# A two-block transformer kernel: modulation chunks of the convolution stage summed on VectorE, and one decay product for each forget head instead of two

## What is computed

```
m = split(silu(c) @ w_mod[1] + b_mod[1], 6)
u = h * (1 + m[1]) + m[0]
b_gate, c_gate, x_in = split(u @ w_in, 3)            # 1024 x 3072
y = (b_gate * conv3(c_gate * x_in)) @ w_out          # 1024 x 1024
h = layer_norm(ALPHA * h + m[2] * y)
f = experts(h * (1 + m[4]) + m[3]);  h = layer_norm(ALPHA * h + m[5] * f)
```

```
cum = cumsum(log_sigmoid(ff + b_f))                  # per head, over tokens
s[t, s'] = q[t].k[s'] / 8 + cum[t] - cum[s']         # then causal softmax, @ v
```

## Time and profile before

| | |
|---|---|
| median of 3 runs | 2254.5 us (2253.36 to 2256.22) |
| profiled execution | 2256.84 us, of which the span of instructions is 2255.0 us |
| mean granted TensorE clock | 0.900 of full |
| TensorE busy | 1791.9 us (79%) |
| VectorE busy | 530.0 us (24%) |
| ScalarE busy | 362.1 us (16%) |
| DMA, mean over the span | 260 GB/s, at most 429 in a slice |

### The profile page before, as it was taken

How to read it: one execution, slowest core, us unless ns; L and a number is a source line. 1 busy time by engine, 2 the same in 40 slices (tenths; PEclk the granted TensorE clock), 3 DMA queues, 4 the chain that set the end, 5 groups by cost and what they waited for, 6 DMA issues and landing times. The chain is left out here.

```text
span 2255.0 us, 27622 instructions
## 1 busy us (share of the span) xinstructions
PE 1791.9 (79%) x11960; PEld 1058.7 (47%) x11960; DVE 530.0 (24%) x1051; ACT 362.1 (16%) x729; POOL 57.5 (3%) x69
## 2 busy tenths in 40 slices
PE   6897666656558977656565569999999999999999
PEld 4454111112017743201111147887588678785785
DVE  0435000001012240100000044242343243413432
ACT  1131000000001010000000012223431022324310
POOL 0000000000000000000000001020000001100000
PEclk8997887878779988878778779999999999999999
DMA  9882999999998567999999943211422232112221
GB/s 405 355 365 84 402 428 428 428 428 428 428 429 372 200 247 313 428 428 428 428 428 422 428 170 141 83 47 65 182 76 87 109 150 76 70 62 112 112 87 45
DMA packets 43503, 586.54 MB, mean 260 GB/s; under 512 B 4913, under 2 KB 5041, under 8 KB 8081
## 3 DMA queue, kind: packets, MB, share of 16 engines
q1 hardware_dynamic: 40464, 574.11, 61.7%
q0 software_dynamic: 2224, 8.31, 0.9%
q10 hardware_dynamic: 720, 2.74, 0.3%
HBM read 584.09 MB, written 1.05 MB: 259 GB/s over the span
## 5 line engine op out<-in xcount | busy, mean ns | idle before, releaser
L1321 PE MATMUL ps<-ring,arena 128*32 128x512 f32 x1536 | 244.6, 769 | 170.2 <-DMA ring<-in_experts 157.4
L1321 PE MATMUL ps<-arena 128*32 128x512 f32 x1536 | 254.8, 801 | 156.5 <-DMA arena<-in_experts 156.5
L1087 PE MATMUL ps<-arena,ring 128*128 128x256 f32 (+3 forms) x1184 | 234.7, 359 | 8.0 <-issue 3.2
L1087 PEld LDWEIGHTS ps<-arena,ring 128*128 128x128 f32 (+2 forms) x1184 | 202.3, 189 | 38.3 <-issue 5.1
L1321 PEld LDWEIGHTS ps<-arena 128*32 128x32 f32 x1536 | 50.3, 130 | 355.9 <-DMA arena<-in_experts 259.0
L1321 PEld LDWEIGHTS ps<-ring,arena 128*32 128x32 f32 x1536 | 48.8, 126 | 351.1 <-DMA ring<-in_experts 220.6
L1417 PE MATMUL ps<-arena,ring 128*128 128x256 f32 x768 | 183.6, 388 | 0.0
L1417 PEld LDWEIGHTS ps<-arena,ring 128*128 128x128 f32 x768 | 142.8, 191 | 29.2 <-issue 9.7
L1440 PE MATMUL ps<-arena,ring 128*128 128x256 f32 x640 | 149.2, 383 | 0.0
L1440 PEld LDWEIGHTS ps<-arena,ring 128*128 128x128 f32 x640 | 121.9, 192 | 26.3 <-issue 10.1
L2064 DVE TENSOR_TENSOR arena<-ps,arena 128x512 f32<-128x512 f32 x16 | 10.3, 686 | 496.6 <-PE ps L1321 496.6
(11 more groups left out here) (331 smaller groups left out, 1898.8 us busy)
## 6 DMA issues: line engine op xcount, KB each, us to landing
ring<-in_experts SPq DMA_DIRECT2D x96, 2048.0 KB, 35.8
arena<-in_experts SPq DMA_DIRECT2D x96, 2048.0 KB, 35.7
ring<-in_stream SPq DMA_DIRECT2D x61, 2048.0 KB, 8.5
arena<-in_stream SPq DMA_DIRECT2D x15, 2048.0 KB, 19.2
ring<-in_stream SPq DMA_DIRECT2D x2, 1696.0 KB, 7.0
gate<-in_b_mod POOLq DMA_DIRECT2D x4, 512.0 KB, 10.8
ring<-in_stream SPq DMA_DIRECT2D x4, 512.0 KB, 4.3
tab<-in_tables_first SPq DMA_DIRECT2D x1, 1729.0 KB, 42.5
```

Source lines behind the costliest of these rows:

```text
L1087: mm = M(dst, lhs(k), rhs(k), start=k == 0, stop=k == n - 1)
L1321: mm = M(bank(b + half)[32 * e:32 * e + 32], x[:, k, 32 * e:32 * e + 32], wk[:, e, half * HALF:(half + 1) * HALF], start=k == 0, stop=k == ...
```

## The change

Two edits that don't touch each other.

**Edit 1, modulation chunks of layer 1's groups `early` and `late`.** `mod_chunk` on TensorE and `mod_part` on ScalarE are gone for these eight chunks. In their place `mod_sum` on VectorE makes `part` = sum over the eight row pieces of piece times condition, in eight instructions of 128x512, each waiting for the one before. `mod_fold` stays, with a matrix of ones. It now marks the tile as consumed. The chunks are put between the projections, in the stream, on TensorE and on VectorE.

**Edit 2, forget heads.** The eight gate rows are doubled (rows 96 to 111). `right` holds -8 cum in the second eight rows and 1 in the first. `left`, in two buffers, has for head u only the rows u and 8+u filled: 8 cum and 1. One matmul `left` x `right` gives 8 (cum[t] - cum[s']). VectorE writes `left` anew for each head, in one instruction on 16 partitions.

```diff
+MOD_BEHIND = (("early", 0, 1), ("early", 1, 2), ("late", 0, 2), ("late", 2, 4), ("late", 4, 6), ("late", 6, 6))
@@ weight_stream
-            modulation("early", 0, 1)
-            for j in (2, 4, 3, 5, 0, 1):
+            for n, j in enumerate((2, 4, 3, 5, 0, 1)):
                 add(("conv_in", j), rows(w["w_conv_in"][0, :, j * HALF:(j + 1) * HALF]))
-                if j == 2:
-                    modulation("early", 1)
-            modulation("late")
+                modulation(*MOD_BEHIND[n])
@@ TensorE, mod_fold
+                summed = g in ("early", "late")
+                pe.wait_ge(*(S("mod_dve").at("sum", l, j, KD - 1) if summed else S("mod_act").at("part", l, j)))
...
+                if summed:
+                    mm.then_inc(used, 1)
@@ TensorE, mixer1
                 turn("mix1", h, 0, ready)
-                mod_chunk(*early[0], fold=False)
                 turned("mix1", 0)
...
                 by_halves(0, slot(first), ut, 1).then_inc(used, 1)
-                mod_chunk(*early[1], fold=False)
-                for c in early:
-                    mod_fold(*c)
+                mod_fold(*early[0])
...
                     mm.then_inc(used, 1)
-                pe.wait_ge(*S("mod_dve").at("gate", *early[-1]))
-                modulation("late")
+                    if n == 2:
+                        pe.wait_ge(*S("mod_dve").at("gate", *early[-1]))
+                    group, first, end = MOD_BEHIND[n]
+                    for c in MOD_GROUPS[group][first:end]:
+                        mod_fold(*c)
@@ VectorE, new
+            def mod_sum(l, j):
+                key = ("mod", l, j)
+                part = parts[mod_half((l, j))]
+                ve.wait_ge(*has_landed(key))
+                before = mod_before((l, j), 2)
+                ve.wait_ge(*(consumed(("mod",) + before) if mod_place(before)[0] in ("early", "late") else S("mod_pe").at("fold", *before)))
+                for k in range(KD):
+                    scale = md["condT"][:, k, 0:1]
+                    if k:
+                        ve.wait_ge(*S("mod_dve").at("sum", l, j, k - 1))
+                        V.scalar_tensor_tensor(out=part, in0=slot(key)[:, k], scalar=scale, in1=part, op0=ALU.mult, op1=ALU.add
+                                               ).then_inc(*S("mod_dve").up("sum", l, j, k))
+                    else:
+                        V.tensor_scalar(part, slot(key)[:, k], scale, None, ALU.mult).then_inc(*S("mod_dve").up("sum", l, j, k))
@@ VectorE, conv1
                 for j in range(8):
+                    if j == 4:
+                        for c in late[1:4]:
+                            mod_sum(*c)
                     ve.wait_ge(*consumed(("conv_in", 4 + j // 4)))
...
+                for c in late[4:]:
+                    mod_sum(*c)
                 ve.wait_ge(*Sv.at("z", 7))
@@ TensorE, attention2, forget heads
-                                sel = T1("ident")[:, FF + u - 8:FF + u - 7]
-                                M(dst, at2["cum"][:, a * P:(a + 1) * P], sel.to_broadcast([P, n]), start=False, stop=False)
-                                mm = M(dst, sel.to_broadcast([P, P]), at2["ncum"][:, 0:n], start=False, stop=True)
+                                if a == 0:
+                                    pe.wait_ge(*Sv.at("left", 1, l, u))
+                                mm = M(dst, at2["left"][:, u % 2, a * P:(a + 1) * P], at2["right"][:, 0:n], start=False, stop=True)
@@ VectorE, forget_gate
-                    V.memset(at2["cum"], 0.0).then_inc(*Sv.up("zero", l, 0))
-                    V.memset(at2["ncum"], 0.0).then_inc(*Sv.up("zero", l, 1))
+                    V.memset(at2["right"], 0.0).then_inc(*Sv.up("zero", l))
...
-                    V.tensor_scalar(at2["cum"][rows], f[:, 3], 8.0, None, ALU.mult).then_inc(*Sv.up("cum", l))
-                    V.tensor_scalar(at2["ncum"][rows], f[:, 3], -8.0, None, ALU.mult).then_inc(*Sv.up("ncum", l))
+                    V.tensor_scalar(at2["right"][rows], f[:, 3], right[:, 0:1], right[:, 1:2], ALU.mult, ALU.add).then_inc(*Sv.up("right", l))
@@ VectorE, attention2
+                def left(u):
+                    ve.wait_ge(*Sv.at("left_zero", l, u % 2))
+                    V.tensor_scalar(at2["left"][rows, u % 2], at2["ff"][rows, 3], T2("with_cum", second_at)[rows, u - 8:u - 7],
+                                    T2("with_one", second_at)[rows, u - 8:u - 7], ALU.mult, ALU.add).then_inc(*Sv.up("left", *K, u))
+                for i in range(2):
+                    V.memset(at2["left"][:, i], 0.0).then_inc(*Sv.up("left_zero", l, i))
+                for u in (8, 9):
+                    left(u)
...
                         V.tensor_scalar(st[:, c:c + 2], st[:, 16:18], -1.0, None, ALU.mult).then_inc(*Sv.up("max", *K, u))
+                        if 8 <= u < 14:
+                            left(u + 2)
```

More of the change, by code:

```diff
@@ L139, in second_tables @@
         _put(parts, at, f"level{n}", (i // (2 * b) == t // (2 * b)) & (i // b + 1 == t // b))
+    row = np.arange(P)[:, None]
+    _put(parts, at, "with_cum", 8.0 * (row == FF + np.arange(H2)[None]))
+    _put(parts, at, "with_one", 1.0 * (row == FF + H2 + np.arange(H2)[None]))
+    _put(parts, at, "right", np.concatenate([-8.0 * (row >= FF + H2), 1.0 * (row // H2 == FF // H2)], 1))
     _put(parts, at, "carry", np.repeat((np.arange(2 * T)[None] % CH != 0), P, 0))
@@ L174, in param_columns @@
         fb = g("fox_b_f")
[L175 removed]
+        col(f"fb{layer}", None if fb is None else np.concatenate([np.zeros(FF, np.float32), fb, fb]), 1, FF + 2 * H2)
         col(f"fq_g{layer}", two(g("fox_q_g")), 1)
@@ L512, in two_block_program @@
         at2.update(xn=sc.take(512), t1=sc.take(512), t2=sc.take(512), score=sc.take(768, 2), prob=sc.take(768, 2),
-                   prob_t=sc.take(768, 2), stat=sc.take(64), cum=sc.take(256), ncum=sc.take(256))
+                   prob_t=sc.take(768, 2), stat=sc.take(64), right=sc.take(256))
+        at2["left"] = at2["sq"][:, :, 0:T]
         at2["ff"] = Scratch(ff_at).take(1024, 4)
@@ L990, in _ @@
             ffn(0)
-            def conv_opening(a):
-                if a:
-                    mod_part(*MOD_GROUPS["early"][0])
-                modulated("mix1", m1["ut"], 1, 0)(a)
-            post_norm(0, 1, conv_opening)
-            mod_part(*MOD_GROUPS["early"][1])
+            post_norm(0, 1, modulated("mix1", m1["ut"], 1, 0))
             for j in range(8):
@@ L1002, in _ @@
                   ).then_inc(*S("conv_act").up("c", j))
-            for c in MOD_GROUPS["late"]:
-                mod_part(*c)
             post_norm(1, 0, modulated("ffn1", ff["ut"], 1, 2))
@@ L1031, in mod_fold @@
                         pe.wait_ge(*S("mod_dve").at("gate", *MOD_GATES[i - 1]))
-                    mm = M(bank(mod_row((l, j))), T1("sum_row0"), part, start=True, stop=True)
+                    mm = M(bank(mod_row((l, j))), T1("ones" if summed else "sum_row0"), part, start=True, stop=True)
                 else:
@@ L1036, in mod_fold @@
                         o = MOD_COLUMNS[g] * HALF + (c * KD + half * 4 + i) * 2
-                        mm = M(ps_t[:, o:o + 2], part[:, i * P:(i + 1) * P], T1("sum_cols"), start=True, stop=True)
-                mm.then_inc(*S("mod_pe").up("fold", l, j))
+                        mm = M(ps_t[:, o:o + 2], part[:, i * P:(i + 1) * P], T1("ones")[:, 0:2] if summed else T1("sum_cols"), start=True, stop=True)
+                if summed:
+                    mm.then_inc(used, 1)
+                else:
+                    mm.then_inc(*S("mod_pe").up("fold", l, j))
             def mod_chunk(l, j, fold=True):
@@ L2004, in conv1 @@
                 for j in range(8):
+                    if j == 4:
+                        for c in late[0:2]:
+                            mod_gate(*c)
+                        mod_columns(1, "late", 2, 3)
                     ve.wait_ge(*consumed(("conv_in", j // 4)))
@@ L2346, in attention2 @@
                 K = (1, l)
+                rows = slice(FF, FF + 2 * H2)
+                def left(u):
[6 more added lines that the diff above has]
+                    left(u)
                 for u in range(18):
@@ L2397, in _ @@
             for c in MOD_GROUPS["early"]:
+                mod_sum(*c)
+            mod_sum(*MOD_GROUPS["late"][0])
+            for c in MOD_GROUPS["early"]:
                 mod_gate(*c)
             conv1()
-            for c in MOD_GROUPS["late"][0:2]:
-                mod_gate(*c)
-            mod_columns(1, "late", 2, 3)
             post_norm(1, 0, mixed(1), modulated("ffn1", ff["ut"], 1, 2))
```

31 lines of the change are left out of this document (16 added, 15 removed).

## The result

| | before | changed |
|---|---|---|
| median | 2254.26 us (2253.3 to 2256.22, 6 runs) | 2244.39 us (2241.25 to 2245.53, 6 runs) |
| profiled execution | 2256.84 us, span 2255.0 | 2241.25 us, span 2239.5 |

The ratio is 0.9947, 95% interval 0.9936 to 0.9957: 12 us faster by the ratio, 10 by the medians, where the prediction had 19.7. The profiled execution is the fastest of the six. It is 15.6 us under before's, and 1.4 of these were there ahead of the first changed instruction (the last down projection of layer 0 starts at 666.84 and not at 668.22).

The account below looks back on a forecast made before the run. TensorE was taken to set the pace where both edits lie (DMA paces the experts). Edit 1 at -11.1 and edit 2 at -8.6 gave -19.7 us, from a median of 2254.5 to 2234.8, say 2235; range 2229.5 to 2242.

Parts of the forecast that it names:

- edit 1, the stretch: Opening's last projection half to `mix_out`: chunks go, folds stay, `mix` is bare; 90.73 becomes 78.5 us, 12.3 less.
- edit 1, clock at the opening: Convolution stage's opening: without the chunk the first half-projection may run partly at 1.2 GHz; +1.2 us, bounds 0 and 4.0.
- edit 2, `left` at two entrances: Attention entrance: two memsets and two `left` ahead of head 0's mask lengthen TensorE's wait by 1.2 a layer, +2.4 us.
- edit 2, forget gate: `forget_gate`: one memset and one of two scalings go, the other gains a scalar; 0.35 us a layer back, -0.7.
- Rivals (c) to (e): Late sums make VectorE the bound, 2244 (0.05); slower than before, 2263 (0.03); nothing, saved time is a wait elsewhere (0.02).
- L1768 costs 0.33 and 0.54, 0.87 for a head: Forget heads: the removed matmul's cost by distance of starts, for both query blocks; sixteen heads in two layers, 13.9 us.
- The lower bound, 0.65 from the bare streaming time: Forget heads: bound on the removed matmuls' saving from the fill's 0.2155 for 256 columns; 10.4 us in all.
- `left` pushes the reciprocal by 0.22: Forget heads: `left` between maxima and reciprocal becomes a TensorE wait; six heads in two layers, +2.6 us, bounds 0 and 4.9.
- a forget head of more than 6 us: Sign of being wrong; forecast heads take 5.6 us without `left` on VectorE and 5.8 with it.
- the clock fell behind a wait of 1.87 in layer 1 and not in layer 0; +1.0: Attention entrance: with a 3.1 us wait the clock falls in layer 0 too, at about two in three; 0 to 1.5.
- Rival (b): VectorE paces the forget heads, with longer entrances and a cold spell in layer 0: edit 2 gives -4.2, 2239 us; chance 0.12.
- Rival (a): The convolution stage's opening stays cold: the first half costs 4.0 more and not 1.2, 2237.5 us; chance 0.15.

Follow-up runs that it names:

- e5: e4's kernel plus the first early chunk's eight products as dead work at the convolution stage's opening: 2229.99 us, ratio 0.9883.
- e3: The changed kernel run once more, beside each edit alone on the same chip: 2246.41 us, ratio 0.9950 against the kernel before.
- e1: The kernel before with edit 1 alone: 2244.95 us, ratio 0.9948.
- e4: The changed kernel with the writes of `left` moved: first two and zeroings ahead of the entrance, others behind the probabilities' scaling: 2235.44 us, ratio 0.9897 against before.
- e9: The changed kernel with `left` written on all 128 partitions instead of 96 to 111: 2241.70 us, ratio 0.9938 against before.
- e2: The kernel before with edit 2 alone: 2256.74 us, ratio 0.9997.
- e8: The changed kernel without the semaphore wait on the instruction that writes `left` in heads 8 to 13: 2246.42 us, ratio 0.9956 against before.
- e10: The changed kernel with no wait between `left` and the reciprocal, `left` still on partitions 96 to 111: 2245.43 us, ratio 0.9952 against before.
- e6: The changed kernel plus seven dead products at the attention entrance of both layers: 2239.68 us, ratio 0.9922 against before.
- e11: The changed kernel with `left` on all 128 partitions and no wait between it and the reciprocal: 2243.50 us, ratio 0.9942 against before.
- e7: e4's kernel plus the dead chunk at the opening and four dead products at each attention entrance: 2229.39 us, ratio 0.9875 against before.

## Why the prediction was right and wrong

| step, us in all | forecast | found |
|---|---|---|
| edit 1, the stretch | -12.3 | -12.98 |
| edit 1, clock at the opening | +1.2 | +1.95, and 2.1 in e5 |
| edit 2, one matmul for two | -13.9 | -10.5 |
| edit 2, `left` in twelve heads | +2.6 | +4.3 |
| edit 2, `left` at two entrances | +2.4 | +2.9 |
| edit 2, clock at the entrances | +1.0 | 0 in the profiled execution, +4.3 in e3 |
| edit 2, forget gate | -0.7 | -0.7 |
| sum | -19.7 | -15.0, and -10.7 with e3's clock |

The profiled execution was 15.6 us under the one before, 1.4 of it ahead of the change: 14.2 against the -15.0 of its rows.

**Edit 1** went as told: no fold waited, one bare `mix` of 1.51, DMA hidden at a share of 0.89. Rivals (c) to (e) are out: 5.91 us a sum is far under 8.4, and the stage's gain arrived in the total (e1). The stretch came out shorter since the folds cost 0.81 to 0.89 each, at the lower bound of mine (0.88). The sums were 5.91 us and not 5.55, and the room that I had found for them took it: the first one ended at 702.16, 1.5 us ahead of its fold. The spell at the opening cost 1.95 and not 1.2. I had taken 1.2 as near the one spell at hand, 1.5 us in the fill of layer 1's entrance. That spell was a partial one: the scores ahead of the fill had lost another 0.2, and here the half ran for 4 us at the low clock.

**The step that failed: "L1768 costs 0.33 and 0.54, 0.87 for a head".** I read the distance behind the first matmul of the pair and took it for what goes. But the one that stays costs just such a distance, 0.42 and 0.54; why it does was not tested. What went is what the second of the pair cost, 0.32 and 0.43, less 0.09. The lower bound, 0.65 from the bare streaming time, was the right number: 0.66 found, and 5.80 for 6.46 in each head of e4. This is 3.4 us.

**The step "`left` pushes the reciprocal by 0.22".** It pushed it by 0.45, of which 0.36 became a wait of TensorE (2.17 us a layer between e4's stretch and the changed kernel's, in six heads). The 0.22 counted on an overlap that an instruction on partitions 96 to 111 does not get. On all partitions it pushes by 0.20 (e9), close to the number forecast. This is 1.7 us. The prediction named a forget head of more than 6 us as a sign of its being wrong, and a head with `left` took 6.17. At the entrance the same holds cost 0.4 of the 1.45.

**The step "the clock fell behind a wait of 1.87 in layer 1 and not in layer 0; +1.0".** The case was seen, its chance and its price were too low. With a wait of 3.32 us both layers fall in e2, e3, e8 and e10, for 2.8 to 3.1 us each where the price forecast was 1.5, because the transposes and scores are slow too. The kernel before had paid 1.7 in layer 1, so it is about +4.3 for such an execution. e6 takes it back and shows that this price is real. The changed kernel's own profiled execution paid only what before paid, so its profile alone would have hidden this term. An estimate of its mean, from the executions counted at the end of this document: 2.3 us an entrance behind the longer wait and 0.6 behind that of 1.87, so +3.3 for both layers. That makes -11.7 in all, where the ratio has -11.9, and -0.7 for edit 2 alone, where e2's ratio has -0.7.

Without the first two errors the forecast would have been -14.6, 2239.9, inside the range. The clock term took the time out of it. The term at the opening came out 0.8 too small and the stretch 0.7 too long, and these two cancelled by luck. Rival (b) named the right place, VectorE in the forget heads and at the entrance, and its 2239 missed by the same two terms, the clock and the 0.87. Rival (a) had the right place at the opening but a price twice too high: the clock came up 4 us into the first half. Whether transposes alone bring it up stays open. Here 1.97 us of them did not, but idle time of 3.66 us stands behind them; in e5 it came up under the dead chunk.

**Still open:** why the same wait at the entrance is followed by a fall of the clock in some executions and not in others. Only one length of filling was tried on either kernel.

## What to carry to other kernels

The gain of merging two short matmuls was here the cost of the one that goes, measured behind it (0.75 us a head) less 0.09, and not the distance from the first to the second (0.87). Where two bounds are at hand, say what speaks for each before choosing the higher one. An instruction that is added on an engine with a quarter of load is dear where TensorE waits for the very chain that it joins: place it behind the last link of the chain (e4: 11 us for moving twenty instructions), and start its operands on the partition on which its neighbours start. And work that is taken out of a gap may have brought the clock up: the opening's chunk looked free to remove, and its removal cost 2 us.

## What the hardware did unexpectedly

The same entrance, with the same work ahead of it, kept the full clock or lost it from one execution to the next. With a wait of 1.87 us (before, e1, e4, e5, two layers each) it lost 1.7 us in three cases of eight and nothing in five. With 2.9 to 3.3 us (after, e2, e3, e8, e9, e10, e11) it lost nothing in two of fourteen, 1.5 to 1.7 in three and 2.8 to 3.1 in nine. Filled, in e6 and e7, it lost nothing in four of four. So such a wait is priced as a mean over executions, and one profile shows one draw of it. The opening was another matter: it was slow in all nine executions without a chunk.

An instruction of VectorE on 16 of 128 partitions took as long as one on all (0.42 and 0.41 us for 256 elements), and cost its neighbours 0.25 us more. Two of them in a row, both from partition 96, did not hold each other.
